# A seam between two matrix products: the output projection and the up projection as one program

## The reference

```python
mix = jnp.concatenate([o_fox.astype(x.dtype), o_gdn.astype(x.dtype)], axis=-1)
h = x + jnp.einsum('bte,ed->btd', mix, w_o)
hn = rmsnorm(h, norm_ffn_w)
up = jnp.einsum('btd,df->btf', hn, w_up)
uhist = jnp.concatenate([ffn_conv_hist.astype(up.dtype), up], axis=1)
uc = causal_dwconv(uhist, ffn_conv_w) + ffn_conv_b
gate, val = jnp.split(uc, 2, axis=-1)
h = h + jnp.einsum('btf,fd->btd', jax.nn.silu(gate) * val, w_down)
```

## Time and profile before

| | us |
|---|---|
| median of 3 runs | 3954.78 |
| lowest, highest | 3954.70, 3954.92 |
| the profiled execution | 3959.77 |
| its span in the trace | 3958.1 |
| PE busy in the span | 3749.1 |
| DVE, ACT, POOL busy | 1625.0, 1195.4, 332.6 |

### The profile page before, as it was taken

The page is one execution under the profiler, slowest core; times in us unless marked ns, Lnnn a source line. Parts: engine busy times, 40 slices in busy tenths (PEclk is TensorE's granted clock), DMA queues, the critical chain, the costliest instruction groups (busy, mean ns, idle before and its releaser), DMA issues. The chain is left out here.

```text
span 3958.1 us, 55054 instructions
## 1 busy us (share of the span) xinstructions
PE 3749.1 (95%) x20957; PEld 3247.4 (82%) x20957; DVE 1625.0 (41%) x3498; ACT 1195.4 (30%) x2333; POOL 332.6 (8%) x407
## 2 busy tenths in 40 slices
PE   7999999699999999999998979999999999899998
PEld 7999999577777777676676869999999999688886
DVE  4000477555544554444433434444444444432222
ACT  4112222233333333332212323333333333221111
POOL 3100000211211211111100000000000000000000
PEclk9999999799999999999989989999999999899999
DMA  4221222401221122015433431111111111342222
GB/s 149 69 68 63 62 69 67 90 23 40 54 49 39 34 49 45 18 53 170 143 116 107 128 85 47 44 46 44 46 44 44 46 44 46 106 153 80 81 80 67
DMA packets 346870, 277.73 MB, mean 70 GB/s; under 512 B 117554, under 2 KB 312482, under 8 KB 346615
## 3 DMA queue, kind: packets, MB, share of 16 engines
q1 hardware_dynamic: 333007, 256.13, 22.0%
q0 software_dynamic: 5040, 18.09, 1.3%
q10 hardware_dynamic: 8652, 1.14, 0.3%
HBM read 189.65 MB, written 85.65 MB: 70 GB/s over the span
## 5 line engine op out<-in xcount | busy, mean ns | idle before, releaser
L2415 PE MATMUL bank<-hn_hi,up_w_parts 128*128 128x436 f32 (+1 forms) x3520 | 981.8, 360 | 10.1 <-DVE up_w_parts L2490 10.1
L2415 PEld LDWEIGHTS bank<-hn_hi,up_w_parts 128*128 128x128 f32 x3520 | 662.1, 188 | 42.1 <-issue 10.2
L2415 PE MATMUL bank<-hn_lo,up_w_parts 128*128 128x436 f32 (+1 forms) x1760 | 632.9, 360 | 0.0
L2415 PEld LDWEIGHTS bank<-hn_lo,up_w_parts 128*128 128x128 f32 x1760 | 331.4, 188 | 19.2
L332 PE MATMUL bank<-proj_wh,proj_xh 128*128 128x256 f32 (+1 forms) x1088 | 309.5, 285 | 0.0
L332 PE MATMUL bank<-proj_wl,proj_xh 128*128 128x256 f32 (+1 forms) x1088 | 306.7, 282 | 0.0
L332 PE MATMUL bank<-proj_wh,proj_xl 128*128 128x256 f32 (+1 forms) x1088 | 306.6, 282 | 0.0
L2461 ACT COPY up_raw<-bank 128x436 f32<-128x436 f32 (+1 forms) x220 | 110.3, 502 | 642.3 <-PE bank L2415 612.3
L1436 PE MATMUL bank<-heads_p_pT,heads_p_v 128*65 128x512 f32 (+3 forms) x640 | 289.4, 534 | 10.7 <-issue 10.1
L2486 DVE TENSOR_SCALAR up_hist<-up_raw 128x2 f32 (+2 forms) x264 | 44.9, 170 | 551.3 <-ACT up_acc L2465 547.6
L2655 PE MATMUL bank<-down_w_hi,down_g_hi 128*128 (+1 forms) x748 | 231.5, 391 | 14.4 <-DVE down_g_lo L2719 14.4
(11 more groups left out here) (413 smaller groups left out, 6792.0 us busy)
## 6 DMA issues: line engine op xcount, KB each, us to landing
up_w<-in_w_up_dram SPq DMA_DIRECT2D x44, 512.0 KB, 4.8
down_g_raw<-scratch_g SPq DMA_DIRECT2D x110, 192.0 KB, 2.3
scratch_g<-up_acc SPq DMA_DIRECT2D x88, 218.0 KB, 2.0
heads_s_k<-in_cache_fox_k_dram SPq DMA_DIRECT2D x8, 2048.0 KB, 13.3
heads_s_v<-in_cache_fox_v_dram SPq DMA_DIRECT2D x8, 2048.0 KB, 8.3
heads_d_qkvT<-scratch_gch SPq DMA_DIRECT2D x17, 768.0 KB, 5.6
down_y<-in_w_down_dram SPq DMA_DIRECT2D x22, 512.0 KB, 3.6
scratch_gch<-proj_work SPq DMA_DIRECT2D x48, 218.0 KB, 1.9
```

The costliest lines, as they stand in the source:

```text
L2415: mm = pe.matmul(bank[:, pair(n) + e, 0:width], w_parts[:, a, part, e, k, :], x[:, k, cols], start=(k == 0 and m == 0), stop=(k == KD - 1 ...
```

## The change

`mix` and `ffn_up` become one phase, `mix_and_up`, with one set of semaphores and no close or barrier between them.

- w_o is held in halves by output columns, `wo_hi[n]` and `wo_lo[n]`, each split by two instructions of 512 columns for one of 1024.
- The first 14 tiles are multiplied as before. For the last two (15 and 16) `last_products` does both n = 0 units first, then both n = 1 units: (15,0), (16,0), (15,1), (16,1). Tile 14's transposes stand two k into (16,0). After the n = 0 units w_o's first half is free.
- up's tiles (`w_parts0`, `w`, `state_rows`, `vec_rows`, `vecs`, `raw`, `acc`, `w_parts1`) lie over w_o's places. `load_setup` on SP waits for the n = 0 units, then issues 3 + 4 small loads and the first tile of w_up; all this stands ahead of the load of x of tile 16 and the stores of h of tiles 15 and 16.
- The state is loaded as four groups of rows, so that 11 transposes of 64 partitions do the work of 44 of 16. `turn_setup` stands on PE ahead of (16,1); on DVE `setup()` stands ahead of `add_x(15)`, and the first weights' low halves (`first_lo`) between the additions of tiles 15 and 16. On ACT the first weights' high halves stand ahead of `square(15)`.
- up's loop has its first two f written out too. In the first, tile 15's transposes stand ahead of unit (0,1) and tile 16's ahead of (1,0); units of n >= 3 wait for the tiles that they read. ACT and DVE split tiles 15 and 16 behind the first two units' work.
- The credits (`raw_ready` of ACT, `conv_done` of DVE) are now given behind `square(LATE + 1)` and `normalise(LATE + 1)`.
- h's stores count on two semaphores by parity.

```diff
-    w_hi, w_lo = (ph.sb(n, [P, KM, D], F32R) for n in ("w_hi", "w_lo"))
+    for n in range(ND):
+        wo_hi.append(ph.sb(f"wo_hi{n}", [P, KM, BANK], F32R))
+        wo_lo.append(ph.sb(f"wo_lo{n}", [P, KM, BANK], F32R))
...
+            def load_setup():
+
+                sp.wait_ge(s["prod_mm"], ND * NT - 2)
+                sp.dma_start(vec_rows[:, 0, :], io["ffn_conv_w"][:, 0:2].rearrange("l i (k p) -> (l i k) p", p=P)) \
+                    .then_inc(s["rows_loaded"], 16)
...
+                for j in range(JB):
+                    sp.dma_start(state_rows[j * RS:(j + 1) * RS, :], io["ffn_state"][:, j * NI * P:(j + 1) * NI * P]) \
+                        .then_inc(s["rows_loaded"], 16)
+                load(0)
...
+            for t in range(1, NT):
+                if t == NT - 1:
+                    load_setup()
+                load_x(t)
+                store_h(t - 1)
+                if t < NT - 2:
                     load_m(t + 2)
             store_h(NT - 1)
...
+            def last_products():
+
+                pe.wait_ge(s["in_lo"], 2 * LATE + 2)
+                pe.wait_ge(s["h_ready"], ND * (LATE - 1))
+                for n in range(ND):
+                    for t in (LATE, LATE + 1):
+                        if n == 0 and t == LATE + 1:
+                            pe.wait_ge(s["in_lo"], 2 * t + 2)
+                            pe.wait_ge(s["h_ready"], ND * (t - 1))
+                        for k in range(KM):
+                            if n == 0 and t == LATE + 1 and k == 2:
+                                turn_out(LATE - 1)
+                            if n == 1 and t == LATE + 1 and k == 0:
+                                turn_setup()
+                            mm = three(t, n, k)
+                        mm.then_inc(s["prod_mm"], 1)
...
+            pe.sem_inc(s["up_mm"], UNITS)
+            pe.wait_ge(s["setup_ready"], SETUP)
+
+            def body(i, a, last):
+                if not is_first(i, a):
+                    pe.wait_ge(s["w_split"], 2 * i + (a + 2))
+                for n, (col, width, _), unit, _, _ in each_chunk(i, a):
+                    cols = slice(col, col + width)
+                    for e in range(2):
+                        if is_first(i, a):
+                            if (n, e) in ((0, 1), (1, 0)):
+                                turn_out(LATE + n)
+                            if n == 1 and e == 0:
+                                pe.wait_ge(s["h_ready"], ND * NT)
+                            if n == 0:
+                                pe.wait_ge(s["w_split"], e + 1)
+                            elif n >= 3:
+                                pe.wait_ge(s["split_done"], 2 * (LATE - 1 if n == 3 else NT))
+                        pe.wait_ge(s["raw_ready"], 2 * unit + (2 * e + 2))
...
+            split_hi(LATE - 1)
+            for e in range(2):
+                act.wait_ge(s[f"first_w_loaded{e}"], 16)
+                act.wait_ge(s["prod_mm"], ND * NT - 2)
+                nc.scalar.copy(w_parts[0][:, 0, e], w[:, e]).then_inc(s["w_hi_ready"], 1)
+            square(LATE)
+            square(LATE + 1)
+
+            act.sem_inc(s["raw_ready"], BANKS_CREDIT)
...
+            split_lo(LATE - 1)
+            setup()
+            add_x(LATE)
+            first_lo(0)
+            first_lo(1)
+            add_x(LATE + 1)
+            normalise(LATE)
+            normalise(LATE + 1)
```

More of the change, by code:

```diff
@@ L2021, in mix @@
     assert KM == 2 * HB and KD == 2 * HB and ND == 2 and KM == KD
-    hn_hi, hn_lo, hi_raw, lo_raw = (c[n] for n in ("hn_hi", "hn_lo", "hn_hi_raw", "hn_lo_raw"))
-    w_hi, w_lo = (ph.sb(n, [P, KM, D], F32R) for n in ("w_hi", "w_lo"))
+    LATE = NT - 2
+    NF2, H2 = F2 // P, FC - 1
+    NF, RS = NF2 // 2, DB * H2
+    R = RS + H2
+    CK = 436
+    chunks = [(n * CK, CK, False) for n in range(4)] + [(4 * CK, TOK - 4 * CK, True)]
+    TP = SEQ - 4 * CK
+    MIXED = H2 + TP
+    NK, UNITS = len(chunks), 2 * len(chunks)
@@ L2031, in mix @@
-    LATE = NT - 2
+    AW = 4 * BANK
+    rows_rest = raw[:].rearrange("p a b n -> p (a b n)")
+    assert F2 <= 2 * AW + 4 * BANK
+    places = (acc[:].rearrange("p a b n -> p (a b n)"), w[:].rearrange("p e k n -> p (e k n)"), rows_rest)
+    row_parts = [(places[n][0:R, 0:min(F2 - at, AW)], at) for n, at in enumerate((0, AW, 2 * AW)) if at < F2]
+    s = {n: ph.sem(n) for n in (
+        "small_loaded small_turned small_ready m_loaded x_loaded wo_hi_ready wo_split in_mm in_hi in_lo prod_mm h_ready "
+        "squared half_ready ms_ready rs_ready hn_ready out_mm h_stored0 h_stored1 hi_ready split_done "
+        "rows_loaded first_w_loaded0 first_w_loaded1 setup_turned setup_ready w_loaded w_hi_ready w_split up_mm raw_ready conv_step "
+        "conv_done silu_ready g_ready g_stored0 g_stored1 tail_turned tail_read tail_stored").split()}
@@ L2033, in rows @@
+    BANKS_CREDIT = 8
+    SETUP = 4
     def rows(t):
@@ L2193, in _ @@
             copy_in(1)
-            for t in range(NT):
+            for t in range(LATE):
                 if t >= 1:
@@ new lines, in _, with next_hi, body @@
+            for a in range(2):
+                act.sem_inc(s[f"g_stored{a}"], 16)
+            def next_hi(i, a):
+                f = 2 * i + a
+                act.wait_ge(s["w_loaded"], 32 * f)
+                act.wait_ge(s["up_mm"], UNITS * f)
+                nc.scalar.copy(w_parts[a][:, 0], w[:]).then_inc(s["w_hi_ready"], 1)
+            def body(i, a, last):
+                for n, (col, width, _), unit, slot, stores in each_chunk(i, a):
+                    if n == 2 and not last:
+                        next_hi(*((i, 1) if a == 0 else (i + 1, 0)))
+                    act.wait_ge(s[f"g_stored{slot}"], 16 * stores + 16)
+                    for e in range(2):
+                        act.wait_ge(s["up_mm"], unit + (e + 1 + UNITS))
+                        act.wait_ge(s["conv_done"], unit + (e + 1))
+                        src = bank[:, pair(n) + e, 0:width]
+                        for streams, r, _, cols, _ in parts(slot, e, n):
+                            if streams:
+                                ins = nc.scalar.copy(r[:, :, H2:], src[:, cols].rearrange("p (b r) -> p b r", b=DB))
+                            else:
+                                ins = nc.scalar.copy(r[:, H2:], src[:, cols])
+                        ins.then_inc(s["raw_ready"], 1)
+                        at = bass.ds(chan(e, 2 * i + a), 1)
+                        nc.scalar.activation(acc[:, slot, e, 0:width], src, ACT.Identity,
+                                             scale=vecs[:, 2, at], bias=vecs[:, 3, at]).then_inc(s["raw_ready"], 1)
+                        if is_first(i, a) and n == 0:
+                            split_hi(LATE + e)
+                    act.wait_ge(s["conv_done"], unit + 5)
+                    nc.scalar.activation(acc[:, slot, 0, 0:width], acc[:, slot, 0, 0:width], ACT.Silu) \
+                        .then_inc(s["silu_ready"], 1)
@@ L2245, in _ @@
             dve.wait_ge(s["small_ready"], 1)
+            nc.vector.memset(hist[:, :, RS:R], 0.0).then_inc(s["setup_ready"], 1)
             rest_in(1)
-            for t in range(NT):
+            for t in range(LATE):
                 if t >= 1:
```

407 lines of the change are left out of this document (172 added, 235 removed).

## The result

Median of the runs: before 3954.85 us (3954.70 to 3955.03, 4 runs), after **3931.41 us** (3928.56 to 3932.3, 4 runs). The ratio is 0.9941, 95% interval 0.9928 to 0.9954: 23.4 us less, where 26.6 were forecast. The forecast was 3928.2; the time lies at the upper edge of the range (3931.5). The mechanism of the seam held, and the seam gave even more than forecast. But up's products became slower, which I had held to be unlikely.

What follows compares the result with a forecast made beforehand. PE, 95% busy, bounds the kernel; only its idle or slow-clock time, 35 us at the seam, was to be had. Unit (1,0) starting at 2344.6 instead of 2371.2 saves 26.6 us: median 3954.78 becomes 3928.2; range 3925.0 to 3931.5.

Steps and rivals of the forecast that it cites:

- what bounds the seam: Between mix and up: a serial chain ending in ACT's increment behind its last square; first up product at 2331.8, gap 3.4 us.
- when the loads start: SP, after both n = 0 units of tiles 15 and 16: seven small loads issued from 2315.1 on.
- their landing: Small loads into w_o's places: 6 x 0.4 us of issues plus 4.1, PE starting at 2321.6 after waiting 1.3 us.
- the transposes of 64 partitions: PE's setup transposes, 2 + 11 in place of 2 + 44: 1.35 us taken, bounds 1.0 to 2.2.
- The x of tile 16: SP's load behind tile 15's addition: issued 2325.6, landing 3.9 us later; the skill's formula estimated 3.2 us.
- the credit: ACT's raw_ready increment behind tile 16's square, executed only at the square's end, 2331.7; first up product at 2331.8.
- the clock: Up's first units: the gap ahead lowers PE's granted clock, costing 1.7 us, bounds 0 and 2.4.
- tile 16's transposes and the table load: Up's first units: transposes wait 0 to 0.8 us, taken as nothing; a 1.28 us ACT table load adds 0.3 at most.
- the rest of up at 0.198 us a product: Up behind its first units: product spacing unchanged; a spacing over 0.198 us would be a sign of being wrong.
- rival 4: Slower: up's tiles move in SBUF; over 5.0 ns more per product loses the gain, 10 ns gives 3981 us; chance 0.05.
- nothing is to be gained inside it: Up projection's steady state: PE busy 300.00 of 300 us at clock 1.00, so no gain there.
- 5.0 above the median: Profiled execution: forecast 3933.2 us, taken as 5.0 above the median of the runs, hence 3928.2.

Runs made afterwards that it cites:

- the kernel with the late loads: Changed kernel with the small loads and first up tile only after all of mix's products, setup transposes behind the last product: 3945.66 us, ratio 0.9973.
- the credits' kernel: Changed kernel with ACT's raw_ready and DVE's conv_done credits given ahead of the work instead of behind tile 16's square and normalisation: 3930.26 us, ratio 0.9935.

## Why the prediction was right and wrong

Its times are those of the old trace: 3.0 us are to be added to a time after.

- **Right: what bounds the seam.** A serial chain (loads, transposes, setup, addition, x, addition, ACT's credit) was forecast to end last, and it did, released by the instruction that the forecast named. Forecast (1,0): 2344.6; measured 2339.38 + 3.0 = 2342.4. So the seam saved 28.8 and not 26.6. ACT's credit ended the wait although the square did not (see below).
- **Right: when the loads start.** First small load 2315.1 forecast, 2312.06 + 3.0 = 2315.06.
- **Mis-sized: their landing.** The sum had 6.5 us from the first small load to the transposes (2.4 of issues and the old 4.1 from the last issue to PE's start), hence a wait of 1.3. It took 5.39 us (2312.06 to 2317.45) and there was no idle time ahead of the transposes. In the kernel with the late loads, where PE does wait for them, it is 5.42, with 2.9 from the last issue where the sum had 4.1.
- **Right: the transposes of 64 partitions.** 1.13 us (2317.45 to 2318.58) for 1.35. **Setup** 1.2 for 1.2. **The x of tile 16** 3.99 for 3.9; the estimate of 3.2 by the formula of the Trainium skill (DMA: Bandwidth & Descriptors, Anatomy of one DMA), which is fitted for GpSimd's path, was too low for this load from SP's queue.
- **Mis-sized: the credit.** I let it wait for the square's end, 0.8 us behind the addition. The addition ended at 2326.39 and PE started at 2326.59, while ACT's last square had begun at 2326.46 and ran to about 2327.1: the queue had executed the increment before the square was through. Up's first product comes 2.2 us sooner than forecast, and (1,0) with it: some 1.5 come from the loads, the transposes and the additions, 0.7 from the credit. The loads and transposes let (16,1) begin 1.3 sooner too, so they hardly shorten the gap; that it is 2.27 us instead of 3.4 is mostly the credit.
- **Right in size, but not sure to come: the clock.** 1.7 us forecast; up's first two units took 12.79 us, and 11.06 to 11.32 where no gap stood ahead of them, so 1.5 to 1.7. In one trace a gap of 2.16 us cost nothing (11.33 us, 64 bytes ahead of all weights). The forecast priced it from one earlier gap, and that it came in the measured kernel was likely by these traces (9 of 10), not certain.
- **Right: tile 16's transposes and the table load** cost nothing. The load lasts 1.28 us and Silu starts 1.30 behind its start, so the row holds, and the drain that makes it 2.66 us by the Trainium skill (ScalarE: Activation LUTs, What ACT_TABLE_LOAD costs) isn't seen here:

```profile
2342.01 1.28 ACT L2441 ACT_TABLE_LOAD   x1
2343.31 0.57 ACT L2441 ACTIVATE ffn_acc<-ffn_acc 128x436 f32<-128x436 f32 x1
```

- **Wrong: "the rest of up at 0.198 us a product".** This is the step that failed. The sum ends at (1,0) and puts the change of all that follows at nothing; measured were 199.5 ns a product in odd f, 198.5 in the mean, which the prediction itself had named as a sign of being wrong. Up gave 5.9 us back. The mechanism stood among the rivals (rival 4), with a chance of 0.05, since I only asked whether it could eat the whole gain (5.0 ns a product). The experiments show it: 32 bytes of padding take the 5.8 us away again. At 1.1 ns on the mean it is a term of the sum, and should have stood there with both signs: the table spans -0.9 to +2.2 ns against before, by 5280 products -5 to +11 us. "No row ties that duration to a place" was no reason for zero, only for a bound. That the odd slot would lie elsewhere against `hn` was to be had blind, since the addresses follow from the order of allocation; what a place costs was not.
- **Wrong: "nothing is to be gained inside it"**. PE busy throughout at clock 1.00 is not yet its best spacing: the kernel before, with both slots at 128, gets through up 4.7 us sooner.
- **Wrong: "5.0 above the median" carried over as a constant.** It was 0.9 above the median after, and 1.5 when the kernel before was run again. It belongs to one execution: that first profile's stages ahead of w_o were 3.0 us longer than after's. The reference should have been the median alone, with the difference of the traces taken off.

The account: 26.6 forecast, +2.2 in the seam, -5.9 in up, +1.6 behind it, makes 24.5 in the traces; the medians show 23.4, and the last 1.1 is within what runs of one kernel differ by.

## What to carry to other kernels

Where a change moves the place in SBUF of the stationary operand of a stage that PE bounds, write a term for it with both signs, and try pads of 32 to 224 bytes: here the best place was worth 10.4 us against the changed kernel's (4.5 against the places before), more than a third of what rewriting the seam brought. At a seam between two stages look at what is merely bookkeeping: a credit placed behind the last useful instruction cost 4 us, as it stood behind a chain that nothing of the next stage needed. And compare traces in lengths between two instructions that both have, not in whole spans.

## What the runs showed of the hardware that was not expected

- The spacing of f32 products (fp32r operands, 436 columns, 128x128 weights) depends on how the weights' tile lies against the moving operand's, by the distance of their starts in a partition modulo 256 bytes: 196.5 ns at 128, 197.4 at 0, 199.5 at 224. Moving both together by 32 bytes changes nothing, moving the weights' slot by 256 neither. The other slot's place adds up to 1.2 ns, and the chunks of one slot differ by up to 7.6 ns (193.8 to 201.4 at 160); the mechanism is open. It shows in mix too (227.8 and 233.3 ns a product, 217.6 and 221.4 us).
- ACT's queue executes an increment of a semaphore that stands alone behind an ACTIVATE before that has ended: PE started 0.13 us after the start of a square of 0.62 us, and 0.13 to 0.14 in each of the eleven traces with the late credit.
- Nine gaps in PE of 2.07 to 2.37 us brought the granted clock to 0.58 to 0.61 in the next 4.11 us, which cost 1.5 to 1.7 us on top; a tenth, of 2.16 us, left it at 1.00. 1.1 us of thin transposes without a gap left it at 1.00 (window of the credits' kernel above).
- The stages ahead of w_o, the same in all kernels, ended up to 9 us apart from trace to trace (2101.7 to 2110.4), more than most edits here were worth.
